# Feed-forward fed with the unnormalised residual, squares and halves made tile by tile, y stored in quarters

## The reference, cut to what matters

```
x = x + mixed @ w_o
h2 = rmsnorm(x, g_ffn)            # x * rsqrt(mean(x*x) + 1e-6) * g
x = x + (silu(h2 @ w_gate) * (h2 @ w_up)) @ w_down      # D_FF = 5632
y = rmsnorm(x, g_final)
```

## Time and profile before

| what | us |
|---|---|
| median of 3 timed runs | 2242.05 (2241.3 to 2242.24) |
| the profiled execution, its own time | 2239.98 |
| its span, first to last instruction | 2237.8 |
| PE busy | 2086.7 (93%) |
| DVE busy | 1007.9 (45%) |
| ACT busy | 738.5 (33%) |
| chain that ended last: PE, DVE, DMA | 85%, 7%, 3% |

### The profile page before, as it was taken

How to read it: one execution, slowest core, us unless ns; L and a number is a source line. 1 busy time by engine, 2 the same in 40 slices (tenths; PEclk the granted TensorE clock), 3 DMA queues, 4 the chain that set the end, 5 groups by cost and what they waited for, 6 DMA issues and landing times.

```text
span 2237.8 us, 38450 instructions
## 1 busy us (share of the span) xinstructions
PE 2086.7 (93%) x15718; PEld 1862.7 (83%) x15718; DVE 1007.9 (45%) x1161; ACT 738.5 (33%) x953; POOL 36.8 (2%) x59
## 2 busy tenths in 40 slices
PE   5999967999998989988998997999999999999996
PEld 4999745658885855558998997999999999999995
DVE  4454966717665601024454344444444444333333
ACT  3333202352323200023443233444454444233332
POOL 0000002100000000000000000000000000000000
PEclk9999987899998998888999998999999999999998
DMA  5444353324531399973445452444444444554452
GB/s 190 158 167 152 111 187 98 84 87 142 176 125 66 105 379 362 369 287 113 169 165 196 145 198 91 160 164 166 169 169 165 160 164 167 172 167 160 163 168 81
DMA packets 96821, 375.69 MB, mean 168 GB/s; under 512 B 27954, under 2 KB 38834, under 8 KB 69234
## 3 DMA queue, kind: packets, MB, share of 16 engines
q1 hardware_dynamic: 70626, 335.36, 43.0%
q10 hardware_dynamic: 21152, 19.66, 2.7%
q0 software_dynamic: 4976, 19.71, 2.5%
HBM read 358.14 MB, written 16.53 MB: 167 GB/s over the span
## 4 chain that ended last, share of the span: by engine, by line
PE 85%; DVE 7%; DMA 3%; ACT 2%; issue 2%; SPq 2%; ACTq 0%; POOL 0%; DVEq 0%; POOLq 0%
PE ps L420 13%; PE ps L912 13%; PE ps L913 13%; PE ps L914 12%; PE ps L871 5%; PE ps L872 4%; PE ps L873 4%; PE ps L454 2%; PE ps L455 2%; PE ps L456 2%; PE ps L812 2%; PE ps L844 1%; DMA gram<-arena 1%; PE ps L856 1%; PE ps L576 1%
## 5 line engine op out<-in xcount | busy, mean ns | idle before, releaser
L1766 DVE TENSOR_TENSOR weights_lo<-ring,weights_hi 128x2048 fp32r<-128x2048 f32 (+1 forms) x152 | 305.5, 2010 | 466.2 <-ACT weights_hi L1314 466.2
L912 PE MATMUL ps<-h_hi,weights_hi 128*128 128x288 f32 x1408 | 415.4, 295 | 15.4 <-DVE h_lo L1775 15.4
L913 PE MATMUL ps<-h_lo,weights_hi 128*128 128x288 f32 x1408 | 416.9, 296 | 0.0
L914 PE MATMUL ps<-h_hi,weights_lo 128*128 128x288 f32 x1408 | 413.3, 294 | 0.0
L420 PE MATMUL ps<-hT,ring 128*128 128x288 f32 x1472 | 381.2, 412 | 1.2 <-ACT arena L1083 1.2
L1314 ACT ACTIVATE weights_hi<-ring 128x2048 fp32r<-128x2048 f32 (+1 forms) x152 | 257.0, 1691 | 342.5 <-PE ps L914 341.0
L420 PEld LDWEIGHTS ps<-hT,ring 128*128 128x128 f32 x1472 | 273.8, 191 | 79.8 <-issue 7.0
L912 PEld LDWEIGHTS ps<-h_hi,weights_hi 128*128 128x128 f32 x1408 | 265.0, 188 | 15.8 <-DVEq L1790 15.8
L914 PEld LDWEIGHTS ps<-h_hi,weights_lo 128*128 128x128 f32 x1408 | 265.8, 189 | 0.0
L913 PEld LDWEIGHTS ps<-h_lo,weights_hi 128*128 128x128 f32 x1408 | 265.2, 188 | 0.0
L912 PE MATMUL ps<-act_hi,weights_hi 128*128 128x288 f32 x704 | 209.1, 297 | 4.9 <-DVE act_lo L1800 4.9
(11 more groups left out here) (333 smaller groups left out, 3041.0 us busy)
## 6 DMA issues: line engine op xcount, KB each, us to landing
ring<-in_wst SPq DMA_DIRECT2D x201, 1024.0 KB, 4.8
ring<-in_wdn SPq DMA_DIRECT2D x64, 704.0 KB, 4.0
arena<-in_kT SPq DMA_DIRECT2D x64, 512.0 KB, 5.5
arena<-in_v SPq DMA_DIRECT2D x64, 512.0 KB, 6.0
ring<-in_wst ACTq DMA_DIRECT2D x8, 1024.0 KB, 7.9
arena<-chunk_ar_bk ACTq DMA_DIRECT2D x24, 256.0 KB, 3.5
arena<-in_ki SPq DMA_DIRECT2D x64, 64.0 KB, 1.8
chunk_ar_bk<-arena POOLq DMA_DIRECT2D x2, 2048.0 KB, 14.3
```

What stands on the lines that cost most here:

```text
L912: mm(out, W_HI[:, (u - U_FF) % 2, w], hi, start=start, stop=False)
L913: mm(out, W_HI[:, (u - U_FF) % 2, w], lo, start=False, stop=False)
L914: return mm(out, W_LO[:, u % 4, w], hi, start=False, stop=stop)
L1766: tt(W_LO[:, u % 4, 0:m], raw, W_HI[:, at, 0:m].bitcast(F32), ALU.subtract).then_inc(sem("w_split"), 1)
```

## The change

- X1 gets memory of its own in the arena. The reload of x goes to `XA` over hT, and DVE writes X1 = XA + product.
- In the output projection each tile is finished at once: after the residual add DVE makes the low weights, ACT writes `H_HI` = X1 times g (a Copy with scale g) and the square of X1, DVE writes `H_LO` = X1*g - H_HI and adds the square to a running sum `SQS`. The loops over tiles on ACT and DVE are written out.
- PE starts gate unit 0 directly after the output projection, waiting tile by tile for `h_split`. The sum over partitions is now one product with `SQS`, behind that unit.
- 1/rms (`RS`) is applied by DVE to each gate and up product (`GT`, `UT`), before Silu and before the product. The low half of an up unit's successor is made behind the product of Silu and up instead of ahead of it.
- The gate and up products use the banks in the order 2, 3, 0, 1, the down products banks 4 and 5. The down stage starts without waiting for all of A_LO: its first tile waits a quarter at a time.
- In the down stage each tile's square, its part in the running sum and XG = XF times g_final (ACT) are made as the tile is finished. After the reciprocal DVE multiplies three quarters of XG by RS (128x1152 each) and POOL the fourth; SP stores y as four transfers.

```diff
-        SQ2 = area(0, KT, NT)
-        X1 = XF = hT[:, :, 0:NT]
+        XG = area(0, KT, NT)
+        XA = XF = hT[:, :, 0:NT]
+        X1 = area(7168, KT, NT)
+        SQT, SQS = area(34304, 2, NT), area(34880, NT)
+        RS, GT, UT = SG[:, 0, :], SG[:, 1, :], small[:, 2 * NT:3 * NT]
-        H_HI, ... = over("h_hi", "arena", 25600, ...), over("h_lo", "hT", 0, ...)
+        H_HI, ... = over("h_hi", "arena", 0, ...), over("h_lo", "hT", 0, ...)
 ...
 SP
-            sp.wait_ge(sem("y_done"), 1)
-            sp.dma_start(o_y, SQ2).then_inc(sem("y_out"), 16)
+            for g, name, n in ((0, "y_done", 1), (1, "y_done", 2), (3, "y_last", 1), (2, "y_done", 3)):
+                sp.wait_ge(sem(name), n)
+                sp.dma_start(o_y[:, 4 * g:4 * g + 4, :], XG[:, 4 * g:4 * g + 4, :]).then_inc(sem("y_out"), 16)
 ...
 TensorE
-            total_squares(1, SQ2)
+            def squares_total(n):
+                pe.wait_ge(sem("squares_added"), n * (KT - 1))
+                mm(ps[7][:, 0:NT], ones, SQS, start=True, stop=True).then_inc(sem("squares_summed"), 1)
+            gate_up(0, 0, True)
+            squares_total(1)
+            for s in range(1, 4):
+                gate_up(0, s)
+            with pe.Fori(1, FT // 2) as i:
+                for s in range(4):
+                    gate_up(i, s)
-            pe.wait_ge(sem("ff_free"), FT + 2)
-            pe.wait_ge(sem("act_lo"), FT + 2)
+            down(0, 0, True)      # waits act_lo >= 2 + 11 * (q + 1) ahead of each of its four units
 ...
 ScalarE
+            for m in range(KT):
+                u = U_O + m
+                act.wait_ge(sem("unit_read"), u + 1)
+                if u + 2 < U_FF:
+                    mix_high(u + 2)
+                else:
+                    high(u + 2)
+                act.wait_ge(sem("o_free"), 2 + m + 1)
+                fn(H_HI[:, m, :], X1[:, m, :], ACT.Copy, scale=p_("g_ffn", m)).then_inc(sem("h_high"), 1)
+                squared(m, X1[:, m, :], 0)
             act.wait_ge(sem("mean_sq"), 2)
-            fn(SG[:, 0, :], SG[:, 0, :], ACT.Sqrt).then_inc(sem("root"), 1)
+            fn(RS, RS, ACT.Sqrt).then_inc(sem("root"), 1)
+            act.wait_ge(sem("x1_out"), 16 * 4)
 ...
+            for m in range(KT):
+                for u in range(U_DOWN + 4 * m, U_DOWN + 4 * m + 4):
+                    act.wait_ge(sem("unit_read"), u + 1)
+                    if u + 2 < U_END:
+                        high(u + 2, n=FQ * P)
+                act.wait_ge(sem("down_free"), 2 + m + 1)
+                squared(m, XF[:, m, :], 1)
+                fn(XG[:, m, :], XF[:, m, :], ACT.Copy, scale=p_("g_final", m)).then_inc(sem("weighted"), 1)
 ...
 VectorE
+            for m in range(KT):
+                u = U_O + m
+                dve.wait_ge(sem("unit_read"), u + 1)
+                tt(X1[:, m, :], XA[:, m, :], ps[m % 2][:, 0:NT], ALU.add).then_inc(sem("o_free"), 1)
+                ...  # mix_low(u + 2) or low(u + 2)
+                dve.wait_ge(sem("h_high"), m + 1)
+                stt(H_LO[:, m, 0:NT], X1[:, m, :], p_("g_ffn", m), H_HI[:, m, :].bitcast(F32), ALU.mult,
+                    ALU.subtract).then_inc(sem("h_split"), 1)
+                square_added(m, 0)
 ...
             def product(i, t, n=KT * P):
+                dve.wait_ge(sem("unit_read"), i * 4 + (U_FF + 2 * t + 1))
+                tt(GT, ps[(2 * t + 2) % 4][:, 0:NT], RS, ALU.mult).then_inc(sem("scaled"), 1)
                 low(U_FF + 2 * t + 2, i * 4 + (2 * t + 3), 0, n)
-                low(U_FF + 2 * t + 3, i * 4 + (2 * t + 4), 1, n)
+                dve.wait_ge(sem("unit_read"), i * 4 + (U_FF + 2 * t + 2))
+                tt(UT, ps[(2 * t + 3) % 4][:, 0:NT], RS, ALU.mult).then_inc(sem("scaled"), 1)
 ...
-                tt(UG[:, t, :], SIL[:, t, :], ps[2 * t + 1][:, 0:NT], ALU.mult).then_inc(sem("ff_free"), 1)
+                tt(UG[:, t, :], SIL[:, t, :], UT, ALU.mult).then_inc(sem("ff_free"), 1)
+                low(U_FF + 2 * t + 3, i * 4 + (2 * t + 4), 1, n)
 ...
+            for g in range(3):
+                y = XG[:, 4 * g:4 * g + 4, :]
+                tt(y, y, RS.unsqueeze(1).broadcast_to([P, 4, NT]), ALU.mult).then_inc(sem("y_done"), 1)
 GpSimd
+            pool.wait_ge(sem("weighted"), KT)
+            pool.wait_ge(sem("inverse_rms"), 3)
+            y = XG[:, 12:16, :]
+            nc.gpsimd.tensor_tensor(y, y, RS.unsqueeze(1).broadcast_to([P, 4, NT]), ALU.mult).then_inc(
+                sem("y_last"), 1)
```

More of the change, by code:

```diff
@@ L914, in three, with gate_up @@
                 return mm(out, W_LO[:, u % 4, w], hi, start=False, stop=stop)
-            with pe.Fori(0, FT // 2) as i:
-                for s in range(4):
[L918 to L925, removed]
+            def gate_up(i, s, first=False):
+                pe.wait_ge(sem("w_split"), i * 4 + (s + 1))
+                if s % 2 == 0:
+                    pe.wait_ge(sem("ff_free"), i * 2 + (s // 2 + 1))
+                for k in range(KT):
+                    if first:
+                        pe.wait_ge(sem("h_split"), k + 1)
+                    ins = three(ps[(s + 2) % 4][:, 0:NT], U_FF + s, k, H_HI[:, k, :], H_LO[:, k, 0:NT],
+                                k == 0, k == KT - 1)
+                ins.then_inc(sem("unit_read"), 1)
@@ new lines, in _, with down @@
+            gate_up(0, 0, True)
[3 more added lines that the diff above has]
+            with pe.Fori(1, FT // 2) as i:
+                for s in range(4):
+                    gate_up(i, s)
+            def down(i, t, first=False):
+                pe.wait_ge(sem("down_free"), i * 2 + (t + 1))
+                for q in range(4):
+                    if first:
+                        pe.wait_ge(sem("act_lo"), 2 + FQ * (q + 1))
+                    pe.wait_ge(sem("w_split"), i * 8 + (2 * FT + 4 * t + q + 1))
+                    for k in range(FQ):
+                        ins = three(ps[4 + t][:, 0:NT], U_DOWN + 4 * t + q, k, A_HI[:, q * FQ + k, :],
+                                    A_LO[:, q * FQ + k, :], q == 0 and k == 0, q == 3 and k == FQ - 1)
@@ L926, in _ @@
                     ins.then_inc(sem("unit_read"), 1)
-            pe.wait_ge(sem("ff_free"), FT + 2)
-            pe.wait_ge(sem("act_lo"), FT + 2)
-            with pe.Fori(0, KT // 2) as i:
+            down(0, 0, True)
+            down(0, 1)
+            with pe.Fori(1, KT // 2) as i:
                 for t in range(2):
[L931 to L937, removed]
@@ L938, in _ @@
-            total_squares(2, SQ2)
+                    down(i, t)
+            squares_total(2)
         @block.scalar
@@ L1778, in _, with square_added @@
[L1778 to L1790 removed]
+            def square_added(m, phase):
+                dve.wait_ge(sem("tile_squared"), phase * KT + m + 1)
+                if m >= 2:
+                    dve.wait_ge(sem("squares_added"), phase * (KT - 1) + m - 1)
+                if m:
+                    tt(SQS, SQS, SQT[:, m % 2, :], ALU.add).then_inc(sem("squares_added"), 1)
```

110 lines of the change are left out of this document (33 added, 77 removed).

## The result

| | before | changed |
|---|---|---|
| median of 4 runs, us | 2241.68 (2240.98 to 2242.24) | 2199.84 (2198.6 to 2204.99) |
| ratio | | 0.9824, 95% interval 0.9807 to 0.9842 |
| profiled execution: own time / span, us | 2239.98 / 2237.8 | 2200.62 / 2198.8 |

What follows compares the result with a forecast made beforehand. PE, busy for 93% of the span, bounds the kernel, so time goes only where it waits or runs slowly. -26.4 + 3.9 - 14.9 = -37.4 us gives 2202.6, plus 2.07 for the median 2204.6; range 2194 to 2213.

Steps and rivals of the forecast that it cites:

- Seam one: From the output projection's end to the third feed-forward unit: gate unit 0 starts at once, third unit 26.4 us earlier.
- Output projection: Added per-tile work of DVE and ACT stays hidden behind PE with 1.0 us to spare per unit: no cost.
- The rival that binds it to VectorE and ScalarE: In the output projection, hand-overs take the 1.0 us margin and 0.5 more; 16 units lose 8 us: 2212.6, chance 7%.
- Gate and up: The 88 added scalings, 40 us of DVE, stay hidden in this stage: no cost.
- the rival of the pace of down: Matmuls in gate and up fall to the down stage's pace, 5.9 us lost: 2210.5, chance 6%.
- Where down begins: The X1 reload becomes the new wait, ahead of the third down unit's low half: costs 3.9 us.
- F: The end of gate and up, 1920.4 in the trace of before, from which times where down begins are counted.
- The landing of 15.1: Where down begins: the X1 reload takes 15.1 us instead of 11.2, with ring loads running beside it.
- Seam two: From the last matmul to the end of the span: 14.9 us earlier, POOL's quarter hidden if at most 4.1 us.
- The rival of POOL taking turns: At the end, POOL takes turns with DVE and finishes last, up to 4.4 us: 2209, chance 10%.
- The sum: Whole kernel: -26.4 + 3.9 - 14.9 = -37.4 us, a time of 2204.6.
- The slower rival: All 6336 matmuls: new addresses and SBUF traffic slow PE, 5.9 ns each to cancel the gain; 2255 at 8 ns, chance 3%.

Runs made afterwards that it cites:

- gate_after_rms: The changed kernel with the sum of squares ahead of gate unit 0 and PE also waiting for 1/rms before that unit: 2212.42 us, ratio 0.9877.
- sum_before_gate: The changed kernel with the sum of squares put ahead of gate unit 0 on TensorE instead of behind it: 2205.88 us, ratio 0.9836.
- x1_wait_late: The changed kernel with VectorE's wait for the X1 reload moved from the third down unit's low half to the first addition to XF: 2194.74 us, ratio 0.9784.
- ring_loads_held: The changed kernel with SP's loads of the fifth and later down units held until the X1 reload has landed: 2198.95 us in one execution.
- changed_again: The changed kernel itself, run again as a control: 2199.61 us, ratio 0.9813 to the kernel before.

## Why the prediction was right, step by step

- **Seam one**, -26.4: right in size and in mechanism (-26.6). The margin at the last tile of H_LO was 1.2 us (forecast 1.0), PE's loss at the third unit 0.41 (0.35). One reading was wrong and nearly mattered: the stores' 3.8 us are a median of four, and the last of them took 6.6 even before. In the changed kernel it took 6.8, and ScalarE, which waits for it ahead of this chain's table load, was spared by 0.25 us. *gate_after_rms* and *sum_before_gate* found their shares within 0.3.
- **Output projection**, 0: right, 104.5 against 104.4, though VectorE went from 37.64 to 52.78 us of it. The rival that binds it to VectorE and ScalarE is out.
- **Gate and up**, 0: right, +0.4, the rival of the pace of down would be +5.9. The 88 scalings raise VectorE to 271 of 545 us, hidden.
- **Where down begins**, +3.9, measured +2.5: the new wait is the one named, and *x1_wait_late* shows it. That the first two down units follow without a gap, by F+8.8, failed: PE lost 1.9 us to `down_free`. The landing of 15.1 was too long by 2.3; with 11.7 to 15.0 us in kernels alike at this place, hitting it would have been luck. So PE idled 4.2 us and not the 9 forecast, and the slow start behind it was dearer than the 6.0 us of a unit taken from before: 22 matmuls at granted clock 0.50 instead of 12 (stretches of the changed kernel from the third unit's first matmul):

```profile
1907.00:1912.40 5.40, 5.39 (x22) 5.40 (x23) 1.40 (x1) 0.00 (x0) 0.00 (x0) 0.50 0.01 2
1912.40:1914.00 1.60, 1.60 (x14) 1.60 (x14) 0.00 (x0) 0.00 (x0) 0.00 (x0) 1.00 0.00 0
```

  The unit took 7.0. From F: low half at 13.4 (forecast 15.8), PE at 15.2 (17.6), unit read at 22.2 (23.6). The 1.9 us of `down_free` cost nothing here, since the third unit starts by the reload, whenever the first two end; they count once the reload is out of the way.
- **Seam two**, -14.9: the mis-sized term, -12.9. The step that failed is the three products at 1.35 each with POOL's hidden behind them if under 4.1. POOL's was under 4.1 (3.71; the 2.7 estimated for it alone was right, 2.60), but it took its time out of VectorE's: 6.31 for 4.05. So the last store was issued 11.7 us behind the last matmul and not 9.8. The rival of POOL taking turns had the right mechanism and the wrong victim: VectorE, not POOL, finished last, for 2.3 us and not 4.4 (which for POOL at 8.83 should have read 4.7).
- **The sum**: -37.4 against -39.0 of span. The measured terms are -26.6 + 2.5 - 12.9 + 0.5 = -36.5; the other 2.5 lie ahead of the output projection. That the sum is within 0.9 of -36.5 is partly luck: 2.0 too much in seam two and 1.4 too little where down begins cancel. The median came out 4.8 below 2204.6: 2.0 by the profiled own times, and 2.8 because the changed kernel's median is 0.8 below its profiled execution, where that of before is 2.07 above, and neither offset says anything of the change.
- The slower rival would have needed 5.9 ns more a matmul; the rest of down took 268.4 us both times.

## What to carry to other kernels

A factor that is constant along the contraction can be applied to the product, and then the stage behind need not wait for it; here 10 of 27 us came from that overlap and the other 16 are put down to the work that it made needless. When one wait is removed, put the next one as late as its data is used: the same `wait_ge` cost 6 to 7 us in front of a low half and nothing in front of the add that needed it, and a bare increment queued behind unrelated work cost 1.9 and 2.8 us. Don't split an elementwise tail of two-input products between VectorE and GpSimd without looking at both of their durations together.

## What the runs showed of the hardware that was not expected

- Two-input products of VectorE and GpSimd took turns: 1.35 and 2.60 us alone; side by side 3.76 for the one of VectorE's that met GpSimd's, and 3.71 for GpSimd's.
- A 2304 KB reload issued by GpSimd landed after 11.7 to 15.0 us in kernels alike at this place. Where PE waits for it, that goes into the time. Whether the runs' spread comes from it is open: the changed kernel's was 6.4 us where the kernel before had 1.3, but in the later sets that one spread over 15 to 18 as well.
- How many matmuls PE runs at the 1.2 GHz level behind an idle time didn't follow from its length: 22 after 4.2 us in the changed kernel, 12 after 4.2 in *ring_loads_held*, 24 after 3.7 in *changed_again*, 12 after 5.0 in the earlier trace rows. Between 22 and 12 that made 1.0 us at this place.
- A 576 KB store took 3.8 us when it was issued just after a 1 MB ring load had landed (three of the four before, within 0.1 us), and 6.6 to 7.5 when it was issued 0.6 us behind the issue of one (the fourth before, all four in the changed kernel). It was hidden, the last by 0.25 us.
